# Making y in the other two corners of TensorE's array, beside the Z and S products of the chunk steps

## The reference

```
def step(state, inp):
    r_t, w_t, k_t, v_t, kk_t, b_t = inp
    sa = jnp.einsum('bhvk,bhk->bhv', state, -kk_t)
    state = state * w_t[:, :, None, :] + sa[..., None] * b_t[:, :, None, :] + v_t[..., None] * k_t[:, :, None, :]
    return state, jnp.einsum('bhvk,bhk->bhv', state, r_t)
...
_, y = lax.scan(step, state0, xs)
mu = jnp.mean(y, -1, keepdims=True)
var = jnp.mean(jnp.square(y - mu), -1, keepdims=True)
y = ((y - mu) * lax.rsqrt(var + GN_EPS)).reshape(B, S, D_R) * g_lnx + b_lnx
```

## Time and profile before

| | us |
|---|---|
| median of 3 runs | 1141.22 |
| lowest, highest | 1140.84, 1144.06 |
| profiled execution, span from first to last instruction | 1137.1 |
| PE busy in it | 1111.9 (98%) |
| DVE busy | 815.2 (72%) |
| ACT busy | 567.5 (50%) |
| POOL busy | 54.9 (5%) |

### The profile page before, as it was taken

The page is one execution under the profiler, slowest core; times in us unless marked ns, Lnnn a source line. Parts: engine busy times, 40 slices in busy tenths (PEclk is TensorE's granted clock), DMA queues, the critical chain, the costliest instruction groups (busy, mean ns, idle before and its releaser), DMA issues.

```text
span 1137.1 us, 29793 instructions
## 1 busy us (share of the span) xinstructions
PE 1111.9 (98%) x12544; PEld 1013.6 (89%) x12544; DVE 815.2 (72%) x1483; ACT 567.5 (50%) x984; POOL 54.9 (5%) x49
## 2 busy tenths in 40 slices
PE   8999999999999999999999999999999999999996
PEld 8888989898898899998898889888889988999985
DVE  2678786868576877774557886878785778777745
ACT  3644554545454565553246445546453545555531
POOL 0000000000000100000010000000000000000000
PEclk9999999999999999999999999999999999999998
DMA  8533222222375565556464322222224645555651
GB/s 294 167 103 113 71 90 76 86 76 86 131 246 181 167 198 187 187 188 205 139 228 145 113 90 90 85 77 86 76 77 162 229 148 201 193 192 189 202 191 57
DMA packets 45516, 165.44 MB, mean 145 GB/s; under 512 B 5168, under 2 KB 5424, under 8 KB 45136
## 3 DMA queue, kind: packets, MB, share of 16 engines
q1 hardware_dynamic: 42736, 154.03, 40.9%
q0 software_dynamic: 1504, 7.47, 2.2%
q10 hardware_dynamic: 1152, 2.10, 0.5%
HBM read 160.44 MB, written 3.15 MB: 144 GB/s over the span
## 4 chain that ended last, share of the span: by engine, by line
PE 84%; DVE 10%; ACT 2%; POOL 2%; issue 1%; DMA 0%; DVEq 0%; SPq 0%; ACTq 0%
PE ps L741 21%; PE ps L742 19%; PE ps L743 19%; PE ps L898 10%; PE ps L1056 3%; PE ps L716 2%; POOL g L679 1%; PE ps L1114 1%; PE ps L1130 1%; DVE ring_r L1658 1%; PE ps L858 1%; PE ps L839 1%; PE ps L779 1%; DVE X_Y L1780 1%; DVE keep L2194 1%
## 5 line engine op out<-in xcount | busy, mean ns | idle before, releaser
L741 PE MATMUL ps<-x_tok_r,mid_hi 128*128 128x256 f32 x576 | 175.7, 305 | 0.5 <-DVE ring_r L1658 0.5
L743 PE MATMUL ps<-x_tok_r,ring_r 128*128 128x256 f32 x576 | 162.2, 282 | 0.0
L742 PE MATMUL ps<-yb_hi,mid_hi 128*128 128x256 f32 x576 | 162.2, 282 | 0.0
L741 PEld LDWEIGHTS ps<-x_tok_r,mid_hi 128*128 128x128 f32 x576 | 108.6, 189 | 9.4 <-issue 1.4
L1256 ACT CAST mid_hi<-ring 128x1024 fp32r<-128x1024 f32 x80 | 83.8, 1048 | 54.3 <-PE ps L743 44.9
L1658 DVE TENSOR_TENSOR ring_r<-ring,mid_hi 128x1024 fp32r<-128x1024 f32 x80 | 96.9, 1211 | 19.2 <-ACT mid_hi L1256 19.0
L742 PEld LDWEIGHTS ps<-yb_hi,mid_hi 128*128 128x128 f32 x576 | 108.9, 189 | 0.7 <-issue 0.7
L743 PEld LDWEIGHTS ps<-x_tok_r,ring_r 128*128 128x128 f32 x576 | 108.9, 189 | 0.0
L1906 DVE TENSOR_TENSOR rs_ks_r<-ring,tha_kkn_r 128x1024 fp32r<-128x1024 f32 x44 | 53.9, 1224 | 21.8 <-ACT tha_kkn_r L1308 21.8
L1906 DVE TENSOR_TENSOR w_lo<-ring,w_hi 128x1024 fp32r<-128x1024 f32 x42 | 51.4, 1224 | 23.1 <-ACT w_hi L1308 23.0
L1906 DVE TENSOR_TENSOR vs_dC_r<-ring,b_k_r 128x1024 fp32r<-128x1024 f32 x44 | 53.7, 1220 | 17.2 <-ACT b_k_r L1308 17.1
(11 more groups left out here) (477 smaller groups left out, 3381.7 us busy)
## 6 DMA issues: line engine op xcount, KB each, us to landing
ring<-stream_dram SPq DMA_DIRECT2D x281, 512.0 KB, 3.4
lora_w<-lora_dram POOLq DMA_DIRECT2D x2, 1536.0 KB, 7.3
W_bt<-rpar_dram POOLq DMA_DIRECT2D x4, 512.0 KB, 5.0
kt_V<-rpar_dram POOLq DMA_DIRECT2D x4, 512.0 KB, 6.4
x_tok<-x_dram SPq DMA_DIRECT2D x2, 512.0 KB, 4.6
v_saved_dram<-vs_dC ACTq DMA_DIRECT2D x4, 256.0 KB, 4.1
x_tok<-x_dram SPq DMA_DIRECT2D x1, 1024.0 KB, 5.6
vf<-v_saved_dram ACTq DMA_DIRECT2D x4, 256.0 KB, 3.4
```

The costliest lines, as they stand in the source:

```text
L741: pe.matmul(dst, lh, rh, start=start, stop=False)
L742: pe.matmul(dst, lh, rl, start=False, stop=False)
L743: return pe.matmul(dst, ll, rh, start=False, stop=stop)
```

## The change

In the steps, y goes to the other two corners. A new helper `crossed` makes a product from half q into the other half. The state part of y of a unit is issued right behind the Z product of that unit; the Q part right behind the S product of that unit. The signals for Z and S are still given by the last product in the own corners. In step 3 the Q part stands alone. The start and stop marks of the accumulation are set to fit. As y now lies with the two heads exchanged, ACT's copy of `rkV` into `yt` becomes two copies, each from one half into the other, and `y_back` turns y in the other corners, which brings the heads back.

```diff
@@ -847,7 +847,7 @@
                     pe.wait_ge(*dve_att(r // GROUPS, f"lh{(r + 1) % GROUPS}"))
                 else:
                     pe.wait_ge(*act_att(r // GROUPS, f"o{GROUPS - 1}"))
-                mm = turned(unit64(6), yt)
+                mm = turned(unit64(6), yt, OTHER)
                 mm.then_inc(*pe_yT.inc(r, "yT"))
@@ -896,6 +896,12 @@
 
                 for q in HEADS:
                     mm = pe.matmul(dst[q], left[q, u, :], right[q], start=start, stop=stop)
+                return mm
+
+            def crossed(dst, left, right, u, start=True, stop=True):
+
+                for q, o in zip(HEADS, OTHER):
+                    mm = pe.matmul(dst[o], left[q, u, :], right[q], start=start, stop=stop)
                 return mm
@@ -1014,10 +1020,13 @@
                     if c:
                         pe.wait_ge(*dve_wkv(r, f"S{c - 1}"))
                     s_old = S[:, (c + 1) % 2, :, :]
+                    y = [unit64(5)[:, u, :] for u in bc(c)]
                     if c:
                         for b, u in enumerate(bc(c)):
                             mm = per_head(step64(2)[:, b, :], a_of, s_old[:, b, :], u)
-                        mm.then_inc(*pe_wkv.inc(r, f"Z{c}"))
+                            if b == GB - 1:
+                                mm.then_inc(*pe_wkv.inc(r, f"Z{c}"))
+                            crossed(y[b], r_of, s_old[:, b, :], u, start=(b == 0), stop=False)
                     fill(14 + 3 * c)
                     pe.wait_ge(*dve_wkv(r, f"Z{c}" if c else f"Y{LEVELS - 1}1"))
                     for b, u in enumerate(bc(c)):
@@ -1028,15 +1037,12 @@
                         prep_v(r + 1)
                         prep_rnT(r + 1)
                     pe.wait_ge(*act_wkv(r, f"Q{c}"))
-                    if c < NCH - 1:
-                        for b, u in enumerate(bc(c)):
+                    for b, u in enumerate(bc(c)):
+                        if c < NCH - 1:
                             mm = per_head(step64(2)[:, b, :], bt, Qs[:, b, :], u)
-                        mm.then_inc(*pe_wkv.inc(r, f"S{c}"))
-                    for b, u in enumerate(bc(c)):
-                        y = unit64(5)[:, u, :]
-                        mm = per_head(y, rb, Qs[:, b, :], u, stop=(c == 0))
-                        if c:
-                            mm = per_head(y, r_of, s_old[:, b, :], u, start=False)
+                            if b == GB - 1:
+                                mm.then_inc(*pe_wkv.inc(r, f"S{c}"))
+                        mm = crossed(y[b], rb, Qs[:, b, :], u, start=(c == 0), stop=(c == 0 or b == GB - 1))
                     mm.then_inc(*pe_wkv.inc(r, f"y{c}"))
                     if g + 1 < GROUPS and c == 0:
                         prep_rnx(r + 1)
@@ -1556,7 +1562,9 @@
                                 act.wait_ge(*dve_y(r - 1, "yb"))
                             act.copy(gT[:, :, :], tok(7)).then_inc(*act_g.inc(r, "g"))
                             act.wait_ge(*pe_wkv(r, "rkV"))
-                            act.copy(yt[:, :, :], unit64(5)).then_inc(*act_wkv.inc(r, "rkV"))
+                            for q, o in zip(HEADS, OTHER):
+                                last = act.copy(yt[o, :, :], unit64(5)[q])
+                            last.then_inc(*act_wkv.inc(r, "rkV"))
```

## The result

| | before | after |
|---|---|---|
| median of the series on one chip, us | 1141.03 (4 runs, 1139.49 to 1144.06) | 1132.43 (4 runs, 1132.39 to 1133.15) |
| profiled execution, span, us | 1137.1 | 1131.0 |
| its own time, us | about 1139.3 (estimate, see below) | 1133.15 |
| PE busy, us | 1111.9 | 1100.1 |
| DVE busy | 815.2 | 815.5 |

The ratio is 0.9923, 95% interval [0.9907, 0.9938]. A second series of six executions on another chip gave 1133.43 against 1140.09, 0.9943 [0.9922, 0.9965]. Over all series the median of before is 1140.8 (56 executions) and that of after 1132.9 (10). The time of the profiled execution of before isn't on record. In every execution with both numbers the time is 2.0 to 2.5 us above the span, most often 2.2 (1139.42 beside 1137.0 for one of before, 1133.15 beside 1131.0 here), so I estimate it as 1137.1 + 2.2 = 1139.3.

What follows compares the result with a forecast made beforehand. PE, 84% of the chain that ended last, was taken to bound the kernel. Rounds preparing a next one and fourth rounds gave 2.04 + 2.25 + 2.24 = 6.5 us; 1141.2 - 6.5 = 1134.7, range 1130.0 to 1138.4, own range 1133.2 to 1136.2.

Steps and rivals of the forecast that it cites:

- Bursts on PE: PE's small matmuls in the steps: 0.62 to 0.39, 0.85 to 0.39, 0.62 to 0.38; 1.36 us a round, 10.9 in all.
- Lost before Z of step 2: First three rounds, layer 0: PE waits for DVE's write of S, losing 0.23 + 0.46; 0.68 us a round remains.
- Layer 1: First three rounds: 0.22 kept before Z of step 2, the sum of y limits the rest; 0.75 us a round.
- Fourth rounds: Last round of each layer, preparing no next one: 1.12 us gained, the last 0.24 lost before the last transposes of y.
- ACT's copy: Copy into yt split in two: 0.48 us more of ACT each, hidden by 0.79 idle; 3.8 us without that cover.
- Sum: Gain over all rounds of both layers: 2.04 + 2.25 + 2.24 = 6.5 us; span 1137.1 to 1130.6.
- carry-over: Start and end outside the profiled span: median of before 4.1 us above it, taken to hold after the change too.
- No overlap: Rival: y products in the other corners wait for the own ones, PE's work stays as it was; 1141.7 us, chance 0.07.
- the slower one: Rival: each of 144 corner changes on PE costs time, 0.05 to 0.10 us; 1151.8 at 0.07, chance 0.04.
- All of it arrives: Rival: state write, sum of y and last chain move with PE, the full 10.9 us comes; 1130.3, chance 0.10.
- weight split took over: Rival: DVE's weight split behind Z of step 3 becomes late, 0.44 lost in six rounds; 1137.3 us, chance 0.14.

Runs made afterwards that it cites:

- the kernel with both reorderings: Changed kernel with DVE's write of S ahead of the last key operations and its sum of y ahead of the last blending of v: 1130.40, again 1129.31 us.
- the reversed order: Against the kernel before: y in the other corners, but behind all S products of the step as before; 1136.72 against 1140.05 us, ratio 0.9968.

## Why the prediction was right, and where it was off

The forecast was 1134.7, the result 1132.4: faster, inside the range, but 0.8 below the forecast's own range (1133.2 to 1136.2). The mechanism was right; several terms were off by little, and what lies outside the rounds was off by more.

- **Bursts on PE: right.** 0.85 to 0.39 and 0.62 to 0.38, and 0.01 to 0.02 for each Z burst, as taken from the earlier trace rows. One size was off: in the first three rounds of a layer step 0 gives 0.17, not 0.23. The burst there is followed by the products of line 839, and these wait for DVE's copy of what they read, a wait that the prediction didn't look at:

```profile
129.89 0.28 DVE L1711 COPY ang<-ps 8x128 f32<-8x128 f32 x1 [0.37 <-PE ps L831]
```
```profile
130.22 1.15 PE L839 MATMUL ps<-ang,const 8*128 8x128 f32 x8
```

  The products start 0.055 us behind the copy's end in all six such rounds, where they started 0.225 behind it before: the slack was 0.17. It cost nothing here, as that gain is lost anyway; only in the kernel with both reorderings is it seen, where a round gives 1.28, not 1.36.
- **Lost before Z of step 2: right.** In layer 0 PE starts at 137.95, with the whole execution 0.28 later at the first round: 137.66 + 0.28 (137.94). A round gave 0.66, 0.66 and 0.68 (0.68 forecast). The wait released by line 1837 is there, 0.55 in layer 0; in layer 1 it is 0.30, less than the 0.4 to 0.7 named for both. Moving that write brought the loss back, which shows it.
- **Layer 1: the mis-sized term.** A round gave 0.64, 0.67 and 0.70 where I had 0.75. Kept up to Z of step 2 was 0.20 to 0.27 (forecast 0.22). But I took the sum of y to have 0.15 - 0.06 of slack. It has none: the delay there is 0.15, in before and after alike, where several waits stand before the product, and 0.06 once this one stands alone. Three times 0.09 is 0.27; the three rounds fell short of the forecast by 0.24 (2.01 against 2.25).
- **Fourth rounds: right.** 1.07 and 1.09 (1.12 forecast). Most of the rest is a weight split: behind Z of step 2 of these rounds the first long matmul starts 0.42 behind the burst's start, not 0.39, since DVE's split of its weight half ends at 301.71 and the weight load starts 0.06 later. The last 0.24 were lost before PE's turning of y: from the first long matmul behind y of step 3 to the turning it is 9.41 us in before and 9.64 after, in both layers and both executions. The wait that the trace names there grew from 0.70 to 0.75 in one execution and, as forecast, 0.94 in the other (the shorter one has the rest of the 0.24 between the matmuls before it):

```profile
320.22 0.97 PE L916 MATMUL ps<-const,yt 64*64 64x64 f32 x26 [0.75 <-DVE yt L1861]
```
```profile
321.20 0.97 PE L916 MATMUL ps<-const,yt 64*64 64x64 f32 x26 [0.94 <-DVE yt L1861]
```

- **ACT's copy: hidden, as said, but the price was mis-sized.** I took 0.48 more for ACT; it is 0.85. That is more than the idle time of 0.79, and the copy for PE was in time only because it now starts 0.05 before the end of the operation ahead of it (116.35 against 116.40). That it cost nothing was partly luck.
- **Sum: 6.5 forecast, 6.2 measured** (2.00 + 2.01 + 2.16). Outside the rounds the two profiled executions differ by +0.28 before the first, +0.44 between the layers' rounds and -0.62 at the end, together 0.1: 1137.1 less 6.1 is 1131.0. The sum for the span was 1130.6.
- **The term that missed most is the carry-over.** I set 4.1 us as lying outside the span, the median of before less the profiled span. What lies outside is 2.0 to 2.5; the other 1.9 or so were that this execution was a quick one. Carrying them over supposes that executions of the changed kernel are as much slower than such a one, and they weren't: the profiled one of the changed kernel took 1133.15, their median is 1132.9. From the estimated time of the profiled execution, 1139.3, the forecast would have been 1139.3 - 6.5 = 1132.8; that this is nearer is no proof of the method, as the next but one point says.
- **The rivals.** No overlap and the slower one (a cost of changing corners) fell with the bursts of 0.39: the changes of corners in one cost at most 0.02 together. All of it arrives would have been 10.9; with the two anchors moved the rounds give 9.8. No weight split took over; the one in the fourth rounds costs 0.03.
- **Open:** over all series the medians differ by 7.9 us (means by 7.5), the rounds by 6.2. Single executions scatter by more than that rest of 1 to 2 us (before's go from 1136.6 to 1144.9). A part of it looks steady: take the result and the ten runs of kernels other than before, add to the span of every execution what the rounds gained in that run's trace, and the mean of the 61 is 1137.2, against 1138.2 for the 52 executions of before with a span on record, with standard errors of 0.2 and 0.25. So about 1 us more than the rounds gain is there, also with the new order in the own corners (1136.9, ten executions); which stretch has it and why stays open.

Against the Trainium skill: the rule weighed in the prediction ("TensorE: Matmul & The Clock Gate", Part 3, What overlaps and what doesn't: a weight load overlaps a running matmul only where the row group differs) isn't what these runs show. S and y beside it use both row groups (the two halves of the partitions) each, and their records start 0.02 apart. The first weight load for y starts at 135.32, while the first S matmul runs from 135.31 to 135.58 by its modelled end. With y in the own corners the same program takes 0.61 instead of 0.39 for a burst.

## What to carry to other kernels

Products of 64 by 64 on half the partitions use one corner of the array each. In these float32 products the four corners worked beside one another, so two units in the other corners beside two in the own ones cost nearly nothing (0.01 to 0.02 us). It held where the two shared the moving operand and, in the reversed order, where they didn't, and with y as far as two units behind its partner in the program. What counted was that each unit had a partner in its burst. What arrives of such a saving is set by the next delivery from another engine: write down for each wait behind the change when the producer ends and what stands before it in its queue, and move the producer ahead of work that nobody waits for (here 3.6 us more of a possible 4.7). Look for such waits behind every burst, not only the ones that the change aims at: one with 0.17 of slack was missed here. And compare spans with spans: the one profiled execution is not the median one.

## What the runs showed of the hardware

- A product in the other corners started ahead of own-corner products that stand before it in the program: y placed behind all eight records of S started 0.03 behind the first of them, ahead of six.
- An ACT copy from PSUM of 64 partitions by 512 into the other half takes 0.58 us, that of 128 by 512 0.59 to 0.60. Such halves don't overlap with what stands before or behind them as whole copies do (each next one starts 0.59 to 0.61 behind, not 0.48).
- From DVE's end to PE's start it is 0.06 us where a single wait stands before the product and 0.15 where several waits do, measured in one place with the one and the other. The products of line 839 behind DVE's copy started 0.055 behind it in six rounds too.
- In thirteen traces, with the same work in these stretches, the first gram products started between 92.50 and 96.27 us, the way from the first layer's normalisation to the next layer's gram products took 279.5 to 281.2, and from the start of the last turning of y of layer 1 to the end 249.8 to 251.8. That is what scatters from execution to execution. Behind that normalisation PE, after waiting 2.1 us for DVE, ran at a mean granted clock of 0.76 over 7 us in nine of them (part of it at the lower level, 1.2 GHz, the rest at 2.4) and at 1.00 in four; the way from there took 279.5 to 281.2 with the one and 280.1 to 280.8 with the other, so the time doesn't follow it.
